# A hybrid decoder step on one core: another order of scaling, storing and loading in its last phase, ten weight chunks staged elsewhere, and sums moved to GpSimd

## The chip, the cores and the metric

The kernel runs on one core of one Trainium2 chip. The metric is the time of one execution in microseconds (us); smaller is better. Before the change three runs gave 2163.30, 2172.09 and 2173.16 us, so the median is 2172.09 us. PE is the matrix engine (TensorE), DVE is VectorE, ACT is ScalarE, POOL is GpSimd, and SP is SyncE, which in this kernel issues the DMAs. PEld is PE's weight load, SPq the queue of SP.

## The reference

One layer of a decoder with two branches on the same normalised input. 2048 new tokens and 8 sampling tokens pass through it. What the change touches is the end of it:

```python
def mixer_layer(x, ...):
    h = rmsnorm(x, g_pre)
    z = h @ w_in                                   # q, kv, z_att, u_pool, z_pool, g_att, g_pool
    o_lat = blocked_causal_mla(q_abs, q_r, pos, ckv_new, kr_new)
    o = jnp.einsum('bshr,rhv->bshv', o_lat, w_uv).reshape(b, L, ATT_WIDTH)
    y_att = (o * jax.nn.silu(z_att)) @ w_o_att
    p, pool_state = pool_mixer(u_pool, pool_hist, pos, w_pool, pool_scale)
    y_pool = (p * jax.nn.silu(z_pool)) @ w_o_pool
    merged = jax.nn.sigmoid(g_att) * y_att + jax.nn.sigmoid(g_pool) * y_pool
    x = x + merged @ w_out
...
y_prompt, y_sample = rmsnorm(xp, g_final), rmsnorm(xs, g_final)
```

D_MODEL is 1024, there are 8 heads of 128, and all is float32.

## The kernel before, in words

The core first makes the latents, queries and attention of all tokens, then the decode step of the 8 sampling tokens. The function `merge`, the subject of the change, does the rest in two further passes and a last one. Every engine has its own list of instructions, run in the order in which they are written; semaphores tie the lists together. Every float32 matrix product is made from three: an operand is split into a high part (a copy by ACT) and a low part (the difference, `split`, by DVE or POOL), and `three_products` multiplies high by high, high by low and low by high. A product over a depth of four blocks of 128 is thus 12 matmuls.

1. A first pass makes the gates and the pooling branch and stores them in memory (`zs`, `sa`, `sp`, `gp`).
2. The pass over **chunks** (variable `c`, five chunks of 412 tokens). A chunk has 24 units, slots 0 to 23. Slots 0 to 15 are the attention output product (kind `OA`, two units for each of eight tiles), slots 16 to 23 the pooling output product (kind `OP`, eight tiles `n`). A unit is 12 matmuls on 412 columns. Beside the units of chunk `c`, the values of chunk `c + 1` are made, a head at a time: a load of the head's latents (`olf`), high part on ACT, low part on POOL (`values_low`), a product of 3 matmuls, and a multiplication by the gate on DVE (`gated`), split in turn (`gat`). They start at slot `UV_AT`, 14, and take ten steps. After each `OP` unit DVE multiplies its result by the gate (`yp_ok`), and then adds the attention half (`m_ok`); SP stores the sum (`store_m`, to `mg`). Weights come three units ahead (`LEAD`), into six buffers.
3. The **join**: `mg` times the output weights, in eight groups `g` of 256 tokens, by one level of Strassen's scheme in Winograd's form, seven products `p` for each group where eight would be plain, and a tail of 8 tokens. `join_order` writes their order: (g,1), (g-1,4), (g-1,3), (g,2), (g,6), (g,5), (g,7) for each group, all of 12 matmuls on 512 columns. The right operands are 28 weight chunks `moved`, kept in SBUF for all groups; each comes by DMA into one of two buffers `moved_f`, and ACT and DVE split it (`high_moved`, `low_moved`). A few come during the last chunks, and from number 18 on after them: 18 and 19 at once, 20 to 27 with the first group's products (`JOIN_MOVED`). The left operands are the four rows `kept` of a group, made from staged rows of `mg` (three DMAs each, four sums on POOL in `staged_sums`, high part on ACT, low part on DVE).

The buffer `y` has two halves, for even and odd groups. `load_x` fills it with the input rows of a group; DVE adds the seven products into it (the first addition into it is at (g,5), line 2637); ACT makes its squares (`squares`, at (g,3)), POOL the inverse root (`rms`), DVE multiplies by it and by the final gain (`scale`, line 2531), and `store_y` stores it. `load_x(g)` needs the half that `store_y(g - 2)` reads, and waits for that store to land. DVE does `scale(g - 2)` at (g,6), SP issues `store_y(g - 2)` when it comes to (g,5) and `load_x(g)` when it comes to (g,7); it comes to a product when the one before it is complete. PE waits, before product (g,4), until ACT has copied the result of (g,7) out of PSUM (line 2330), and ACT waits for the addition of (g,5) before that, since both use the buffer `p1c`.

## Time and profile before

| | us |
|---|---|
| median of the runs | 2172.09 |
| the profiled execution | 2172.92 |
| its span (first to last instruction) | 2171.1 |
| PE busy in the span | 2025.3 |
| DVE, ACT, POOL busy | 1498.9, 1126.4, 511.8 |

The profile is of one execution. A span is the time from its first to its last instruction; here 1.8 us of the execution lie around it. A busy PE is not PE at its peak: its clock has two levels, and "PEclk" is the granted share of the full 2.4 GHz. In the 40 slices of the page PE is busy at nine tenths or more from the second to the 34th and then falls to six to eight tenths, while its clock falls from 9 tenths and more to 8 and 7; each slice is 54.3 us. The join begins at 1893 us.

### The profile page before, as it was taken

How to read it: one execution, taken by the hardware profiler on the slowest of the kernel's cores; microseconds unless marked ns; L12 is line 12 of the kernel's file. 1: busy time of each engine (PE TensorE's matmuls, PEld its weight loads, DVE VectorE, ACT ScalarE, POOL GpSimd, SP SyncE). 2: the span in 40 equal slices, each digit the busy share in tenths (PEclk: the TensorE clock that was granted, in tenths of full speed). 3: DMA queues.
4: the chain of work that ended last, by engine and by line, in shares of the span. 5: the costliest groups of instructions: out<-in, count | busy, mean ns of one | idle time of the engine just before them, and what ended most of it. 6: DMA issues, size and time to landing. Idle time of an engine off the chain costs nothing.

```text
span 2171.1 us, 37204 instructions
## 1 busy us (share of the span) xinstructions
PE 2025.3 (93%) x13077; PEld 1842.4 (85%) x13077; DVE 1498.9 (69%) x3208; ACT 1126.4 (52%) x2271; POOL 511.8 (24%) x647
## 2 busy tenths in 40 slices
PE   7999999999999999999999999999999999866666
PEld 6999888888888886899999999999998999855544
DVE  7877888888878775686687687587666777543333
ACT  5446766565555555556666666656633444332211
POOL 4444444333201102130040031021033111142210
PEclk9999999999999999999999999999999999988788
DMA  8876465344110313567767767768899988643232
GB/s 303 265 218 189 124 199 161 107 116 121 65 49 21 117 59 123 167 216 244 234 208 246 235 194 259 245 188 283 254 295 310 296 262 271 189 125 93 85 98 80
DMA packets 284249, 396.97 MB, mean 183 GB/s; under 512 B 34016, under 2 KB 152680, under 8 KB 283032
## 3 DMA queue, kind: packets, MB, share of 16 engines
q1 hardware_dynamic: 278272, 374.26, 55.7%
q0 software_dynamic: 2304, 12.58, 1.5%
q10 hardware_dynamic: 3488, 7.75, 1.1%
q8 instruction: 105, 1.72, 0.3%
q14 instruction: 80, 0.66, 0.1%
HBM read 295.77 MB, written 98.96 MB: 182 GB/s over the span
## 4 chain that ended last, share of the span: by engine, by line
PE 37%; DVE 10%; issue 7%; ACT 2%; DMA 2%; POOL 1%; SPq 0%; ACTq 0%; DVEq 0%; POOLq 0%
PE b_ps L131 37%; DVE d_wr L93 4%; ACT d_wr L1345 1%; DVE d_gat L93 1%; DVE d_spf L2602 1%; DVE d_saf L2608 1%; DVE d_pool L93 0%; DMA d_staged<-out_mg 0%; DMA d_quarters<-in_w_quarters 0%; DVE d_ht L93 0%; DVE d_pooled L2566 0%; DVE d_moved L93 0%; DMA d_zsf<-out_zs 0%; DMA d_moved_f<-out_w_moved 0%; DVE d_c L2551 0%
## 5 line engine op out<-in xcount | busy, mean ns | idle before, releaser
L93 DVE TENSOR_TENSOR d_wr<-d_ws,d_wr 128x512 fp32r<-128x512 f32 x568 | 429.2, 762 | 233.4 <-ACT d_wr L1345 227.1
L1345 ACT ACTIVATE d_wr<-d_ws 128x512 fp32r<-128x512 f32 x568 | 350.7, 628 | 281.1 <-PE b_ps L131 276.2
L131 PE MATMUL b_ps<-d_ht,d_wr 128*128 128x258 f32 x3072 | 399.1, 284 | 6.9 <-DVE d_wr L93 5.2
L131 PEld LDWEIGHTS b_ps<-d_ht,d_wr 128*128 128x128 f32 x3072 | 380.3, 189 | 13.8 <-DVE d_wr L93 12.2
L759 PE MATMUL b_ps<-kt,k_qs 128*128 128x512 f32 (+2 forms) x1520 | 337.8, 370 | 1.3 <-DVE b_p L1147 1.3
L131 PE MATMUL b_ps<-d_hb,d_wr 128*128 128x258 f32 x2304 | 302.8, 284 | 6.2 <-DVE d_wr L93 4.6
L759 PEld LDWEIGHTS b_ps<-kt,k_qs 128*128 128x128 f32 x1520 | 265.3, 188 | 49.0 <-DVE b_p L1147 4.3
L131 PEld LDWEIGHTS b_ps<-d_hb,d_wr 128*128 128x128 f32 x2304 | 287.5, 189 | 9.3 <-DVE d_wr L93 7.2
L1101 ACT ACTIVATE b_pt<-b_ps 128x512 fp32r<-128x512 f32 x272 | 158.5, 597 | 168.3 <-PE b_ps L1207 115.6
L93 DVE TENSOR_TENSOR b_pt<-b_ps,b_pt 128x512 fp32r<-128x512 f32 x272 | 183.0, 689 | 87.6 <-ACT b_pt L1101 86.5
L131 PE MATMUL b_ps<-d_moved,d_kept 128*128 128x512 f32 x672 | 173.7, 423 | 72.7 <-ACT d_p1c L2330 55.6
L131 PEld LDWEIGHTS b_ps<-d_moved,d_kept 128*128 128x128 f32 x672 | 136.9, 205 | 109.4 <-ACT d_p1c L2330 57.7
L1207 PE MATMUL b_ps<-b_pt,kv 128*128 128x512 f32 x816 | 227.8, 407 | 0.0
L1094 ACT ACTIVATE b_p<-b_p,b_bias 128x1024 f32<-128x1024 f32 (+7 forms) x192 | 171.6, 896 | 60.0 <-DVE b_low L1154 59.1
L131 PE MATMUL b_ps<-d_gat,d_wr 128*128 128x412 f32 x960 | 185.2, 354 | 7.5 <-DVE d_gat L93 7.5
L131 PEld LDWEIGHTS b_ps<-d_gat,d_wr 128*128 128x128 f32 x960 | 181.8, 191 | 10.1 <-issue 8.8
L1207 PEld LDWEIGHTS b_ps<-b_pt,kv 128*128 128x128 f32 x816 | 143.3, 189 | 24.2
L93 POOL TENSOR_TENSOR k_qs<-k_qf,k_qs 128x512 fp32r<-128x512 f32 (+1 forms) x52 | 71.2, 1370 | 358.8 <-issue 202.8
L1198 PE MATMUL b_ps<-ident,b_p 128*128 128x128 f32 x1088 | 149.2, 273 | 3.1 <-DVE b_p L1171 1.5
L1198 PEld LDWEIGHTS b_ps<-ident,b_p 128*128 128x128 f32 x1088 | 128.3, 140 | 25.6 <-DVE b_pt L93 3.2
L1147 DVE TENSOR_SCALAR_CACHE_REDUCE b_p<-b_ps 128x512 f32<-128x512 f32 (+1 forms) x192 | 125.2, 668 | 15.1 <-PE b_ps L759 13.0
L1171 DVE TENSOR_SCALAR b_p<-b_p,b_inverse 128x1024 f32<-128x1024 f32 (+7 forms) x192 | 133.3, 717 | 0.7
(246 smaller groups left out, 2557.5 us busy)
## 6 DMA issues: line engine op xcount, KB each, us to landing
d_ws<-out_w_sums SPq DMA_DIRECT2D x256, 256.0 KB, 3.5
d_ws<-in_w_pairs SPq DMA_DIRECT2D x192, 256.0 KB, 3.1
d_ws<-in_w_last SPq DMA_DIRECT2D x120, 256.0 KB, 4.1
b_quarters<-in_w_pairs SPq DMA_DIRECT2D x16, 1024.0 KB, 7.6
out_w_sums<-b_sums SPq DMA_DIRECT2D x16, 1024.0 KB, 10.0
out_q<-a_qout SPq DMA_DIRECT2D x32, 384.0 KB, 3.9
d_hf<-out_ht SPq DMA_DIRECT2D x32, 258.0 KB, 3.3
out_zs<-d_out SPq DMA_DIRECT2D x32, 258.0 KB, 4.2
```

The source lines that it names most:

```text
L93: return e.tensor_tensor(low, source, high.bitcast(f32), ALU.subtract)
L131: mm = pe.matmul(out, stationary(a, k), moving(b, k), start=first and k == 0 and a + b == 0, stop=last and k == depth - 1 and a == 1, skip ...
L759: mm = pe.matmul(out, qs[:, a, h, :], keep["kt"][:, first:first + size, b, :], start=k == 0, stop=k == len(pairs) - 1)
L1094: act.activation(span, span, ACT.Exp, bias=bias[:, at:at + 1], scale=-1.0 if negated else SCALE, accum_out=total[:, at, part:part + 1]).th ...
L1101: act.activation(pt[n % NPT][:, 0, :], ps_t[n % NTB][:, :], ACT.Copy).then_inc(pt_hi, 1)
L1147: dve.tensor_scalar(out, inp, 1.0, None, ALU.mult, ALU.max, accum_out=top[:, at, c:c + 1]).then_inc(s_sb, 1)
L1171: dve.tensor_scalar(span, span, inverse[:, at:at + 1], None, ALU.mult).then_inc(p_ok, 1)
L1198: mm = pe.transpose(ps_t[n % NTB][:, h * P:h * P + P], weights(u, h, slice(j * P, j * P + P)), ident[:, :])
L1207: mm = pe.matmul(ps_o[u % 2][:, :], kv[:, j, a, :], pt[n % NPT][:, b, :], start=j == 0 and k == 0, stop=j == tiles(u) - 1 and k == 2)
L1345: act.activation(ahead["wr"][s % WR][:, 0, :, :], ahead["ws"][s % WS][:, :, :], ACT.Copy).then_inc(ahead["w_hi"], 1)
L2602: dve.tensor_tensor(gate[:, :], bank[OP_BANK[a]][:, 0:T], gate[:, :], ALU.mult).then_inc(yp_ok, 1)
L2608: dve.tensor_tensor(saf[out_n][:, :], saf[out_n][:, :], gate[:, :], ALU.add).then_inc(m_ok, 1)
```

## The change

- **y and x.** DVE does `scale(g - 1)` at (g,5), in place of `scale(g - 2)` at (g,6). SP issues `store_y(g - 2)` when it comes to (g,1), in place of (g,5), and `load_x(g + 1)` when it comes to (g,4), in place of `load_x(g)` at (g,7). The fourth staged row of the next group is loaded at (g,2), in place of (g,6). POOL does `rms` after all four rows. The tail's load and split come earlier (at (7,2) and (7,6)).
- **Weight chunks.** Chunks 0 to 17 are loaded and split at the odd slots 1 to 11 of the third, fourth and fifth pass over a chunk. The last ten (in the order `RAW_ORDER`) are loaded without `moved_f`, each to a place of its own where `gat` lies, which is free once the last attention unit is done; they are loaded at slots 19 to 23 of the last chunk and split there and at (0,1). The four staged rows of group 0 come earlier.
- **Sums.** The 40 additions of the two gated halves go from DVE to POOL (`gated_sum`), each placed three steps behind a `values_low`; they are stored one slot later.
- **Value steps** begin at slot 13 (`UV_AT`), and the loads for them and the `quarters` loads come one slot earlier.

```diff
-UV_AT = 14
+UV_AT = 13
+RAW_ORDER = (21, 22, 23, 18, 19, 20, 24, 25, 26, 27)
...
-        STORE_M = {unit_slot(c, 20 + n): (c, n) for c in range(NC) for n in range(KD)}
+        STORE_M = {unit_slot(c, 21 + n): (c, n) for c in range(NC) for n in range(KD)}
-        LOAD_MOVED = {unit_slot(2, 4) + 4 * m: m for m in range(16)}
-        LOAD_MOVED |= {unit_slot(NC - 1, 17) + 2 * m: 16 + m for m in range(4)}
+        SPLIT_MOVED = {unit_slot(2 + m // 6, 1 + 2 * (m % 6)): m for m in range(12)}
+        SPLIT_MOVED |= {unit_slot(NC - 1, 1 + 2 * m): 12 + m for m in range(6)}
+        LOAD_MOVED = {s: m for s, m in SPLIT_MOVED.items()}
+        LOAD_STAGED = {unit_slot(NC - 1, at): i for i, at in enumerate((2, 4, 10, 12))}
+        SPLIT_STAGED = {unit_slot(NC - 1, at): i for i, at in enumerate((4, 6, 12, 14))}
+        LOAD_RAW = {unit_slot(NC - 1, 19 + k): (2 * k, 2 * k + 1) for k in range(5)}
+        SPLIT_RAW = {unit_slot(NC - 1, 21): (21,), unit_slot(NC - 1, 22): (22, 23), UNITS - 1: (18, 19, 20, 24)}
+        JOIN_RAW = {(0, 1): (25, 26, 27)}
...
+                if s in LOAD_RAW:
+                    if LOAD_RAW[s][0] == 0:
+                        sp.wait_ge(unit_ok, tile_slot(NC - 1, KD, 0))
+                        sp.wait_ge(moved_ok, MOVED_OK + 18)
+                    for n in LOAD_RAW[s]:
+                        load_raw(RAW_ORDER[n])
...
-            for q in range(2):
-                load_x(q)
+            load_x(0)
             for n, (g, p) in enumerate(JOIN):
                 sp.wait_ge(unit_ok, UNITS + n)
+                if p == 1 and 2 <= g < GROUPS_C:
+                    store_y(g - 2)
+                if p == 4 and 2 <= g + 1 < GROUPS_C:
+                    load_x(g + 1)
+                if (g, p) == (0, 6):
+                    load_x(1)
+                if p == 2 and g + 1 < GROUPS_C:
+                    load_staged(g + 1, 3)
...
-                if p == 5 and 2 <= g:
-                    store_y(g - 2)
-                if p == 7 and 2 <= g:
-                    load_x(g)
...
+            def high_raw(m):
+                act.wait_ge(raw_in, RAW_BASE + 16 * len(RAW_ORDER))
+                act.activation(moved[m][:, 0, :], raw[m][:, :], ACT.Copy).then_inc(moved_hi, 1)
...
+            def gated_sum(c, n):
+                pool.wait_ge(yp_ok, c * KD + n + 1)
+                pool.wait_ge(ya_ok, c * KD + n + 1)
+                pool.tensor_tensor(saf[n][:, :], saf[n][:, :], spf[n % 4][:, :], ALU.add).then_inc(m_ok, 1)
...
+                for h in range(KD + 3):
+                    if c < NC - 1 and h < NH:
                         values_low(c + 1, h)
+                    if h >= 3:
+                        gated_sum(c, h - 3)
...
-                            dve.tensor_tensor(saf[out_n][:, :], saf[out_n][:, :], gate[:, :], ALU.add).then_inc(m_ok, 1)
...
+                if p == 5 and g:
+                    scale(g - 1)
-                if p == 6 and 2 <= g < GROUPS_C:
-                    scale(g - 2)
```

How the rows of an engine move, at three places. The first is SP in the join, in a group in the middle. Before, a row of `mg` (lines 2035 to 2037), then the load of x (2053), the next row, and the store of y (2045):

```order
L2035 DMA d_staged_13156<-out_mg 128x128
L2036 DMA d_staged_13156<-out_mg 128x128
L2037 DMA d_staged_13156<-out_mg 128x256
L2053 DMA d_y_0_13148<-in_x 128x1024
L2053 DMA d_y_1_13149<-in_x 128x1024
L2035 DMA d_staged_13154<-out_mg 128x128
L2036 DMA d_staged_13154<-out_mg 128x128
L2037 DMA d_staged_13154<-out_mg 128x256
L2045 DMA out_y<-d_y_0_13150 128x1024
L2045 DMA out_y<-d_y_1_13151 128x1024
```

The same place after the change, where a row is lines 2049 to 2051, the store line 2059 and the load line 2067:

```order
L2049 DMA d_staged_13166<-out_mg 128x128
L2050 DMA d_staged_13166<-out_mg 128x128
L2051 DMA d_staged_13166<-out_mg 128x256
L2059 DMA out_y<-d_y_0_13160 128x1024
L2059 DMA out_y<-d_y_1_13161 128x1024
L2067 DMA d_y_0_13160<-in_x 128x1024
L2067 DMA d_y_1_13161<-in_x 128x1024
L2049 DMA d_staged_13164<-out_mg 128x128
L2050 DMA d_staged_13164<-out_mg 128x128
L2051 DMA d_staged_13164<-out_mg 128x256
```

The load of x now directly follows the store of the same half, both stand behind the first three rows of a group, and the fourth row stands behind them.

The second place is POOL in a chunk's pooling units. Before, the low parts of the values (line 93) stand alone; after, sums (line 2423) stand between them. Before:

```order
L93 TENSOR_TENSOR d_ols_13072<-d_olf_13081,d_ols_13072 128x412
L93 TENSOR_TENSOR d_ols_13073<-d_olf_13082,d_ols_13073 128x412
L93 TENSOR_TENSOR d_ols_13072<-d_olf_13083,d_ols_13072 128x412
L93 TENSOR_TENSOR d_ols_13073<-d_olf_13084,d_ols_13073 128x412
L2401 TENSOR_TENSOR d_changed<-d_quarters 128x512
```

After:

```order
L2423 TENSOR_TENSOR d_saf_13091<-d_saf_13091,d_spf_13074 128x412
L93 TENSOR_TENSOR d_ols_13072<-d_olf_13081,d_ols_13072 128x412
L2423 TENSOR_TENSOR d_saf_13092<-d_saf_13092,d_spf_13075 128x412
L93 TENSOR_TENSOR d_ols_13073<-d_olf_13082,d_ols_13073 128x412
L2423 TENSOR_TENSOR d_saf_13093<-d_saf_13093,d_spf_13076 128x412
L93 TENSOR_TENSOR d_ols_13072<-d_olf_13083,d_ols_13072 128x412
L2423 TENSOR_TENSOR d_saf_13094<-d_saf_13094,d_spf_13077 128x412
L93 TENSOR_TENSOR d_ols_13073<-d_olf_13084,d_ols_13073 128x412
```

Five of the eight sums of a chunk stand so, and three behind them.

The third place is SP near the end of the last chunk, after the change (line 2022 loads a gate, 2028 stores a sum, 2039 loads a raw weight chunk):

```order
L1338 DMA d_ws_12065<-in_w_last 128x512
L2039 DMA d_raw_13131<-out_w_moved 128x512
L2039 DMA d_raw_13132<-out_w_moved 128x512
L2022 DMA d_spf_13074<-out_sp 128x412
L2039 DMA d_raw_13133<-out_w_moved 128x512
L2039 DMA d_raw_13134<-out_w_moved 128x512
L2022 DMA d_spf_13075<-out_sp 128x412
L2028 DMA out_mg<-d_saf_13091 128x412
L2039 DMA d_raw_13135<-out_w_moved 128x512
L2039 DMA d_raw_13136<-out_w_moved 128x512
```

All ten raw loads stand ahead of the fourth of the eight stores; before, this stretch held single loads of `moved_f`, each of which needs the split of the chunk two before it.

## Rows read from the trace of the kernel before

**Rows 1.** Stretches: length, busy PE, PEld, DVE, ACT, POOL (x), PEclk, DMA share, GB/s
```profile
1826.50:1893.00 66.50, 58.62 (x290) 57.12 (x288) 41.93 (x65) 23.60 (x37) 9.25 (x16) 0.92 0.70 215
1893.00:1934.30 41.30, 24.75 (x85) 18.85 (x85) 14.12 (x21) 11.14 (x18) 8.32 (x16) 0.75 0.48 152
1934.30:1970.70 36.40, 36.39 (x156) 29.17 (x156) 18.70 (x21) 14.50 (x28) 17.80 (x35) 1.00 0.31 80
1970.70:2003.90 33.20, 21.10 (x84) 16.77 (x84) 11.32 (x13) 7.84 (x15) 7.94 (x19) 0.85 0.31 95
2037.30:2143.20 105.90, 63.78 (x240) 50.31 (x240) 32.16 (x39) 20.79 (x43) 18.04 (x44) 0.79 0.30 94
```

**Rows 2.** The chain that ended last, one period of the join (start, us, what)
```profile
1970.70 10.64 issue
1981.34 0.70 DVE d_y L2637
1982.15 0.61 ACT d_p1c L2330
1982.80 21.14 PE b_ps L131 x84
```

**Rows 3.** PE's waits in the join (total us, times, longest)
```profile
PE b_ps L131 <- ACT d_p1c L2330: 55.6, 5, 12.1
PE b_ps L131 <- DVE d_tail L93: 10.1, 1, 10.1
```

**Rows 4.** Timeline of SP's queue around one period of the join
```profile
1993.03 0.33 SPq L2035 DMA_DIRECT2D d_staged<-out_mg  x1
...
2001.53 1.49 SPq L2045 DMA_DIRECT2D out_y<-d_y  x2
...
2008.12 0.90 SPq L2053 DMA_DIRECT2D d_y<-in_x  x2
```

**Rows 5.** Timeline of DVE, same period
```profile
1991.46 2.08 DVE L93 TENSOR_TENSOR d_kept<-d_staged,d_kept 128x896 fp32r<-128x896 f32 x2
...
1999.17 1.09 DVE L93 TENSOR_TENSOR d_kept<-d_staged,d_kept 128x896 fp32r<-128x896 f32 x1 [2.78 <-ACT d_kept L2245]
2000.18 2.47 DVE L2531 SCALAR_TENSOR_TENSOR d_y<-d_y,d_stat,d_gfin 128x1024 f32<-128x1024 f32 x2
2013.88 0.69 DVE L2637 TENSOR_TENSOR d_y<-d_y,d_p1c 128x512 f32<-128x512 f32 x1 [11.23 <-issue]
...
2020.67 0.69 DVE L2644 TENSOR_TENSOR d_y<-d_y,b_ps 128x512 f32<-128x512 f32 x1 [3.87 <-PE b_ps L131]
2023.40 0.69 DVE L2646 TENSOR_TENSOR d_u2c<-d_u2c,b_ps 128x512 f32<-128x512 f32 x1 [2.04 <-PE b_ps L131]
```

**Rows 6.** Timeline of PE in the pass over chunks
```profile
1676.76 1.40 PE L131 MATMUL b_ps<-d_ols,d_wuv 128*128 128x412 f32 x3 [3.33 <-POOL d_ols L93]
...
1705.76 34.04 PE L131 MATMUL b_ps<-d_gat,d_wr 128*128 128x412 f32 x180 [1.50 <-DVE d_gat L93]
...
1767.76 35.48 PE L131 MATMUL b_ps<-d_gat,d_wr 128*128 128x412 f32 x180 [2.27 <-DVE d_gat L93]
```

**Rows 7.** Clock of the stretches after PE's 2.27 us wait (columns as Rows 1)
```profile
1767.70:1772.00 4.30, 4.24 (x15) 4.18 (x16) 1.46 (x3) 0.73 (x2) 0.00 (x0) 0.62 0.90 280
```

**Rows 8.** PE and DVE near the end of the last chunk, timeline
```profile
1878.60 13.79 PE L131 MATMUL b_ps<-d_gpl,d_wr 128*128 128x412 f32 x60 [5.01 <-DVE d_spf L2602]
...
1877.26 0.69 DVE L93 TENSOR_TENSOR d_moved<-d_moved_f,d_moved 128x512 fp32r<-128x512 f32 x1 [5.68 <-ACT d_moved L2239]
```

**Rows 9.** PE at the start of the join, timeline
```profile
1917.30 4.77 PE L131 MATMUL b_ps<-d_moved,d_kept 128*128 128x512 f32 x12 [12.79 <-ACT d_u2c L2327]
```

**Rows 10.** POOL and DVE in pooling units of the fourth chunk, timeline
```profile
1807.71 1.15 POOL L93 TENSOR_TENSOR d_ols<-d_olf,d_ols 128x412 fp32r<-128x412 f32 x1 [2.13 <-ACT d_ols L2230]
...
1807.84 1.47 DVE L2608 TENSOR_TENSOR d_saf<-d_saf,d_spf 128x412 f32<-128x412 f32 x1
...
1815.13 0.58 DVE L2608 TENSOR_TENSOR d_saf<-d_saf,d_spf 128x412 f32<-128x412 f32 x1
```

More of the change, by code:

```diff
@@ L1866, in merge @@
         moved_f = [at(where["gap"] + n * piece, f"moved_f{n}", [P, HALF]) for n in range(2)]
+        raw_at = {m: t_at[0] + (n * piece if n < 3 else 8 * NH * T - (len(RAW_ORDER) - n) * piece)
+                  for n, m in enumerate(RAW_ORDER)}
+        raw = {m: at(first, f"raw{m}", [P, HALF]) for m, first in raw_at.items()}
+        assert raw_at[23] + piece <= raw_at[18]
         gfin = at(where["gap"], "gfin", [P, D])
@@ L1910, in merge @@
         moved_in = [gp_out, sem("moved_in1")]
+        raw_in = moved_in[0]
         MOVED_BASE = (GP_BASE + 16 * NG * NAP, 0)
+        RAW_BASE = MOVED_BASE[0] + 16 * 9
         NG_ALL = NAP * PAIRS
@@ L2025, in load_moved, with load_raw @@
                 sp.dma_start(moved_f[m % 2][:, :], io[source][m % HD, part, :, :]).then_inc(moved_in[m % 2], 16)
+            def load_raw(m):
+                source, part = MOVED[m // HD]
+                sp.dma_start(raw[m][:, :], io[source][m % HD, part, :, :]).then_inc(raw_in, 16)
             def load_staged(q, i):
@@ L2158, in _ @@
+            load_staged(1, 2)
             for n in range(4):
                 sp.wait_ge(m_out[n], M_BASE[n] + 16 * 2 * NC)
[L2160 to L2161 removed]
+            load_x(0)
             for n, (g, p) in enumerate(JOIN):
                 sp.wait_ge(unit_ok, UNITS + n)
[L2164 to L2175 removed]
+                if p == 1 and 2 <= g < GROUPS_C:
[6 more added lines that the diff above has]
+                    load_staged(g + 1, 3)
+                if p == 7 and g + 2 < GROUPS_C:
+                    for i in range(3):
+                        load_staged(g + 2, i)
+                if (g, p) == (0, 7):
@@ L2315, in _ @@
                             high_staged(0, SPLIT_STAGED[s])
-            for m in (18, 19):
-                high_moved(m)
+                        for m in SPLIT_RAW.get(s, ()):
+                            high_raw(m)
             for n, (g, p) in enumerate(JOIN):
@@ L2442, in _ @@
                     change(k)
-                if c < NC - 1:
-                    for h in range(NH):
+                if c == NC - 1:
+                    for i in range(HD):
+                        staged_sums(0, i)
+                for h in range(KD + 3):
+                    if c < NC - 1 and h < NH:
                         values_low(c + 1, h)
+                    if h >= 3:
+                        gated_sum(c, h - 3)
             pool.memset(half_c[:, :], -0.5).then_inc(win_step, 1)
             pool.wait_ge(win_step, done[0] + 1)
-            for i in range(HD):
-                staged_sums(0, i)
-            for g in range(GROUPS_C):
+            for g in range(GROUPS_C + 1):
                 if g + 1 < GROUPS_C:
@@ L2453, in _ @@
                         staged_sums(g + 1, i)
-                        if i == 2 and g >= 2:
-                            rms(P, g % 2, 2, 4 * (g - 1), 3 * (g - 2))
-            for q in range(GROUPS_C - 3, GROUPS_C):
-                if q > GROUPS_C - 4:
-                    rms(P, q % 2, 2, 4 * q + 4, 3 * q)
+                if g:
+                    rms(P, (g - 1) % 2, 2, 4 * g, 3 * (g - 1))
             rms(TAIL_C, 0, 1, 4 * GROUPS_C + 2, 3 * GROUPS_C)
@@ L2512, in low_moved, with low_raw @@
                 split(dve, moved[m][:, 1, :], moved_f[m % 2][:, :], moved[m][:, 0, :]).then_inc(moved_ok, 1)
+            def low_raw(m):
+                dve.wait_ge(moved_hi, MOVED_HI + 18 + RAW_ORDER.index(m) + 1)
+                split(dve, moved[m][:, 1, :], raw[m][:, :], moved[m][:, 0, :]).then_inc(moved_ok, 1)
             def low_staged(q, i):
@@ L2617, in _ @@
                             low_staged(0, SPLIT_STAGED[s])
-            for m in (18, 19):
-                low_moved(m)
+                        for m in SPLIT_RAW.get(s, ()):
+                            low_raw(m)
             for n, (g, p) in enumerate(JOIN):
```

53 lines of the change are left out of this document (18 added, 35 removed).

## The prediction

> **What bounds the kernel now.** I read the page's slices first: PE is busy throughout until about 1850 us, so most of the span is bound by PE, and only the end is loose. The busy times by stretch say how loose: in the join's middle PE works 21 of 33 us at a granted clock of 0.85 and less, while DMA has a share of 0.3 and no other engine is half busy [rows 1]. So nothing is full there; something waits in a ring. The chain that ended last shows the ring, the same for each group: 10.6 us in which nothing visible runs, then DVE's first addition into y, ACT's copy of (g,7), and PE's 84 matmuls [rows 2]. PE's list of waits has five of them, 55.6 us, and a sixth before the tail, 10.1 us [rows 3]. What lies in the unnamed 10.6 us is read from two timelines: DVE scales y at 2000.18, SP stores it at 2001.53, x's load follows at 2008.12 and DVE's waiting addition starts at 2013.88 [rows 4, 5]. Store to load is 6.6 us, load to use 5.8 us: the DMA of y and x is the bound, begun too late for its group.
>
> Before the join, PE in the chunks waits 1.50 us twice and 2.27 us twice for the last low part of `gat` (two of them in the rows), 3.33 us once for POOL [rows 6], and 5.01 us in the last chunk for DVE, which waited 5.68 us for a weight chunk behind one of two `moved_f` buffers [rows 8]. Then 12.79 us at the join's start [rows 9].
>
> **Part 1, y and x (the middle of the join).** First what PE alone needs. Two results that DVE took up as soon as PE had them are 2.73 us apart [rows 5]; the stretch without the ring's wait has 13 products (156 matmuls) in 36.4 us, 2.80 each, at clock 1.00 [rows 1]. I take 2.75, or 19.25 us for a group. The 172.5 us from 1970.7 to 2143.2 hold 408 matmuls: 84 and 240 in the rows and 84 in a stretch between them like the first [rows 1]. That is 34 products, 93.5 us by 2.75. Freed: 79.0 us, and 1.4 us more because the tail's first matmuls, behind a wait too, run slowly.
>
> What is late next? Call the start of (g,1) zero. The scaling ends near 2 us (it stands behind (g-1,5) and takes 2.47 us [rows 5]); the store starts at 1 to 2 us, lands by 8 to 9, the load lands by 14 to 15; it is wanted at 16.5, when (g,5) ends. Slack 2 us. The other ring is the left operands. The fourth row of g+1 may load only when the first is split, 2.4 us after (g-1,3) ends (8.2). Before, from the issue of that load to the end of its low part took 7.2 us (1993.03 to 2000.26) [rows 4, 5], so the end is near 17.9, and PE wants it at 19.25. Slack 1.3 us, but x's load now is in flight beside it: I add 0.5 us a group over six groups, 3 us. The other end is 2 us a group, 12 us; below nothing is excluded, since PE has no less than its products to do. DVE needs about 12.5 us in 19, ACT 9. Part 1: minus 77.4.
>
> **Part 2, the join's start and the last chunk.** From 1893.0 to 1934.3 PE makes seven products in 41.3 us [rows 1]; 19.3 would do, 22.0 freed. SP has the ten raw loads issued before slot 23, so the first group waits for no `moved_f`. New there: ACT's copy of (0,6) stands behind the third staged row, about 1.2 us, and (1,1) needs the fourth row of group 1, which can load only when the first is split, about 2.3 us, with 1.5 us for a slower clock: 5 back, minus 17.0. The last chunk: 288 matmuls at 34.04/180 = 0.189 us [rows 6] are 54.5 of 66.5 us [rows 1], 12.0 freed, of which 3.7 belong to part 3. New: ACT's first raw copy waits for all ten loads. SP sends a pair per unit from the end of slot 16, since the gate loads between them want POOL's sums; the last pair goes about 12 us later and lands 3 to 5 us on, beside the end of slot 23. DVE's multiplication for slots 22 and 23 stands behind those splits, and PE wants it to start the join. 2.5 to 4.5 us; I take 4 with the clock. Its own ends are 0 (loads in time) and 10 (loads as slow as in the busiest stretches). Minus 4.3.
>
> **Part 3, the value steps one slot earlier.** The end of `gat` comes a unit (2.3 us) sooner, and PE waited at most 2.27 us for it: 7.5 us in four waits go. After 2.27 us the clock was 0.62 for 4.3 us [rows 7] and the 180 matmuls took 35.48 instead of 34.04 [rows 6]: 1.4 us more, twice, and a little in the others. Minus 10.5 (3.7 of them in the last chunk). The wait of 3.33 us stays: the `quarters` loads, POOL's work on them and the value steps all move by the same slot.
>
> **Part 4, the sums on POOL.** DVE is freed of 40 additions, and gains PE nothing, since no wait of PE on DVE in the pooling units is left to cut. POOL gets them. No row shows the operation there; the nearest has the same shape and two inputs in SBUF, 1.15 us [rows 10], and I take that. They stand between the low parts of the values, which PE waits for with about 0.4 us to spare. The two engines hinder each other: the addition on DVE that began while POOL worked took 1.47 us, one that did not 0.58 [rows 10], so it stood until POOL was done. If POOL's operations (2 of 1.15) and DVE's two with both inputs in SBUF (0.69 and 0.58) exclude each other in full, a pooling unit needs 3.57 us and PE gives it 2.82 (12 and 3 matmuls). Starts stand closer than durations, 0.5 us apart for one of 0.58, so 3.2 is nearer. 0.4 us over 5 units less 0.4 us spare, four times, is 6 us; I take 5. Ends: 0 (PE's spare takes it all) and 13 (0.75 over 5 units, less the spare, four times). Below nothing is excluded as PE has nothing to win.
>
> The Trainium skill (SBUF — State Buffer, "SBUF: two separate sides") says that this pair of ports is an exclusive lock, held for the whole instruction, between GpSimd and a VectorE operation with two SBUF inputs. By that rule in full, the sum would be the upper end, 13 in place of 5; the row of 1.47 us agrees with the blocking, and no row here shows it for the sums. The skill's GPSIMD Engine Reference, "Engine selection", would leave elementwise sums on VectorE, as about twice as slow on GpSimd; 1.15 beside 0.58 us agrees, but PE does not wait on that difference alone.
>
> **The sum.** Span 2171.1 - 79.0 - 1.4 + 3 - 22.0 + 5 - 8.3 + 4 - 10.5 + 5 = 2066.9. With 1.8 us around the span 2068.7: about 2069, 4.8% less. The profiled execution, 2172.92, lies 0.8 us above the median of the runs, so nothing is to be converted.
>
> **Rivals.**
> A, 2087 us: POOL and DVE exclude each other in all eight pooling units of four chunks, 0.75 us x 32 = 24 in place of 5. For it, [rows 10]; against it, three of eight sums come after the last low part, where PE waits for nothing of POOL.
> B, 2082 us: the row chain and x's load stretch the join's period from 19.75 to 22, over six groups 13.5 us. For it, a slack of 1.3 us and a load of 1 MB beside it; against it, DMA share 0.3 [rows 1].
> C, 2120 us: the wait for x only shrinks. If store and load come one product later than I have them and each lands 3 us later, 8 us of 10.6 stay in each of six periods, 48 us and a lower clock. Against it, 6.6 and 5.8 us were measured with rows of `mg` in flight too.
> D, slower than before: a POOL sum in the value steps takes over 4.8 us. Place: the pooling units of four chunks; price: 1.15 + x - 2.82 us in each of 32 units; at x = 4.8 that is 100 us, the whole of the gain. The nearest rows exclude it nearly: POOL's 1.15, and DVE's longest in these units, 1.47.
> E, about 2048: none of my new waits comes (3 + 5 + 4 + 5 less what the clock gives back) and the 3.33 us wait goes.
>
> **How the numbers follow.** Forecast 0.62; A 0.12; B 0.12; C 0.03; D 0.02; E 0.09. The forecast's time is 2069. The range goes from 2050 (just over E) to 2092 (past A and B), with C, D and part of E left out, as are sums of A and B. A measurement of this kernel tells about 0.5% from nothing, 11 us. All cases but D are far beyond that: faster 0.96, same 0.02, slower 0.02.
>
> **What would show it.** Right: in the join's middle PE runs without a wait over 2 us, at clock 1.00, a period of 19 to 20 us; DVE's first addition into y never waits for a DMA; no wait of PE on `gat`; a wait of some us between slot 22 and the first product of the join, behind raw chunks; POOL's sums near 1.15 us. Wrong: a wait at (g,5) of several us (C); PE waiting for POOL's low parts in each pooling unit (A); PE waiting for `kept` before (g,1) (B). If PE's clock stayed at 1.2 GHz through the join, a product would take 4.8 us as the one after the long wait did [rows 9], and 56 products would give back all that is won; no busy stretch in the rows shows that, so it has no chance of its own.

## The result, and the profile after

The changed kernel took 2078.78 us (median of 4 runs, 2075.72 to 2079.02), the kernel before 2169.73 us beside it (4 runs). The ratio is 0.9581, with a 95% interval of 0.9555 to 0.9607: 4.2% less. The forecast was 2069 us and 4.8% less, so some 10 us are missing by the time and 13 us by the ratio. The profiled execution took 2075.72 us with a span of 2073.9; the prediction's sum for the span was 2066.9, so there 7.0 us are missing. Two single executions understate the miss: the profiled one before took 3.2 us more than its median, and the one after took 3.1 us less.

From the page of the changed kernel, busy times and the clock in 40 slices:

```profile
PE 2003.5 (97%) x13077; PEld 1826.2 (88%) x13077; DVE 1502.1 (72%) x3168; ACT 1123.6 (54%) x2271; POOL 586.5 (28%) x687
PEclk9999999999999999999999999999999999999999
```

PE is now busy for 97% of the span and its clock no longer falls at the end. PE's timeline in the join (start, us, what, waits in brackets) answers to [rows 3, 9]:

```profile
1891.18 13.88 PE L131 MATMUL b_ps<-d_moved,d_kept 128*128 128x512 f32 x48 [5.96 <-DVE d_spf L2638]
1906.81 3.04 PE L131 MATMUL b_ps<-d_moved,d_kept 128*128 128x512 f32 x12 [1.75 <-ACT d_u2c L2352]
1911.23 136.39 PE L131 MATMUL b_ps<-d_moved,d_kept 128*128 128x512 f32 x588 [1.39 <-DVE d_kept L93]
```

The join starts at 1891.18 us. The six long waits are gone: from (1,1) on, 588 matmuls, 49 products, follow each other without one, 2.78 us each. The ring of y as DVE and SP show it in a middle group, to be laid beside [rows 4, 5]:

```profile
1968.85 0.69 DVE L2669 TENSOR_TENSOR d_y<-d_y,d_p1c 128x512 f32<-128x512 f32 x1
1969.45 2.68 DVE L2567 SCALAR_TENSOR_TENSOR d_y<-d_y,d_stat,d_gfin 128x1024 f32<-128x1024 f32 x2
...
1975.52 0.69 DVE L2676 TENSOR_TENSOR d_y<-d_y,b_ps 128x512 f32<-128x512 f32 x1 [2.05 <-PE b_ps L131]
```
```profile
1971.71 0.85 SPq L2059 DMA_DIRECT2D out_y<-d_y  x2
1976.22 0.81 SPq L2067 DMA_DIRECT2D d_y<-in_x  x2
```

The first addition into y (L2669) waits for nothing, where it waited 11.23 us; the scaling stands behind it. The next store of y is issued at 1991.29, so a group takes about 19.5 us.

The two profiles split the span at the join's first product. From there to the end before took 2171.1 - 1893.07 = 278.0 us, after takes 2073.9 - 1891.18 = 182.7: minus 95.3, where the sum had 77.4 + 17.0 = 94.4. Ahead of it the change gained 1.9 us, where the sum had 4.3 + 10.5 - 5 = 9.8. So the whole miss lies ahead of the join. The 1.9 us are no gain of the change at all. The last rows of the pass before the chunks, which the change does not touch, are in the two profiles:

```profile
1572.69 1.70 PE L131 MATMUL b_ps<-d_ht,d_wr 128*128 128x258 f32 x12 [0.57 <-ACT d_p L2269]
```
```profile
1570.33 1.69 PE L131 MATMUL b_ps<-d_ht,d_wr 128*128 128x258 f32 x12 [0.57 <-ACT d_p L2294]
```

The changed kernel's execution was 2.4 us ahead here already. That is the spread of single executions: e6 below has the same instructions up to the join and stands at 1573.30. From these rows to the join's first product is called the pass below; it took 320.4 us before and 320.9 us after, so the pass over chunks gained nothing. PE's waits there, grouped (total us, times, longest), from 1590 to 1911 us of the changed kernel, and the same of the kernel before:

```profile
PE b_ps L131 <- POOL d_ols L93: 10.5, 3, 7.9
PE b_ps L131 <- DVE d_spf L2638: 7.0, 5, 6.0
PE b_ps L131 <- DVE d_wr L93: 2.9, 3, 1.1
PE b_ps L131 <- ACT d_u2c L2352: 1.8, 1, 1.8
PE b_ps L131 <- DVE d_gat L93: 1.3, 4, 0.3
```
```profile
PE b_ps L131 <- DVE d_gat L93: 7.5, 4, 2.3
PE b_ps L131 <- DVE d_spf L2602: 5.7, 2, 5.0
PE b_ps L131 <- POOL d_ols L93: 4.3, 4, 3.3
```

The waits on `gat` went, 6.2 us. In their place stand 6.2 us more on POOL and 2.9 us on weights. The longest of them, where [rows 6] has 3.33:

```profile
1678.29 1.40 PE L131 MATMUL b_ps<-d_ols,d_wuv 128*128 128x412 f32 x3 [7.88 <-POOL d_ols L93]
```

What is behind it is read on POOL, where lines 2432 to 2437 make `changed` from `quarters`, and on SP:

```profile
1652.64 2.94 POOL L2433 TENSOR_TENSOR d_changed<-d_quarters 128x512 f32<-128x512 f32 x1
...
1670.95 1.27 POOL L2432 TENSOR_TENSOR d_changed<-d_quarters 128x512 f32<-128x512 f32 x1 [11.97 <-DMA d_quarters<-in_w_quarters]
...
1676.74 2.52 POOL L93 TENSOR_TENSOR d_ols<-d_olf,d_ols 128x412 fp32r<-128x412 f32 x2
```
```profile
1643.88 0.61 SPq L2156 DMA_DIRECT2D d_quarters<-in_w_quarters  x1
...
1650.27 0.38 SPq L2015 DMA_DIRECT2D d_saf<-out_sa  x1
1659.01 0.37 SPq L2161 DMA_DIRECT2D out_w_moved<-d_changed  x1
1659.43 2.15 SPq L1338 DMA_DIRECT2D d_ws<-in_w_last  x1
...
1663.05 0.38 SPq L2156 DMA_DIRECT2D d_quarters<-in_w_quarters  x1
```

It is a ring of its own, `quarters` load, POOL's four operations, store, next load, and only then the low parts of the values, which stand behind it on POOL. The slots of the load and the store are lower bounds: SP reached the third load at 1643.88, the kernel before issued it at 1644.03 (its row: `1644.03 0.38 SPq L2142 ... d_quarters`). Counted from the start of the pass (1570.33 and 1572.69), the third load came 2.2 us later than before (73.6 against 71.3) though its slot is one earlier, the fourth 4.8 us later, and the low part began 3.9 us later (1676.74 after, 1675.21 before). PE wanted it 0.7 us earlier (at 1678.29 - 7.88 = 1670.41 after, 1676.76 - 3.33 = 1673.43 before). Together these are the 4.55 us by which the wait grew. While SP stood at the store, from 1650.7 to 1659.0, the weight loads behind it stood too; no wait of PE for weights is seen between 1638 and 1678 us. The chain that ended last names the link, in both kernels:

```profile
1663.05 7.83 DMA d_quarters<-in_w_quarters
```
```profile
1660.61 8.64 DMA d_quarters<-in_w_quarters
```

### The profile page after: what moved, and what is told of

Its sections match the earlier page's. It is cut to its first block, busy times and chain, and to the rows that moved or that the text cites. A ratio compares the mean times of both kernels' runs of the same rounds, so it can differ in the third digit from the quotient of the medians.

```text
span 2073.9 us, 37208 instructions
## 1 busy us (share of the span) xinstructions
PE 2003.5 (97%) x13077; PEld 1826.2 (88%) x13077; DVE 1502.1 (72%) x3168; ACT 1123.6 (54%) x2271; POOL 586.5 (28%) x687
## 4 chain that ended last, share of the span: by engine, by line
PE 36%; DVE 10%; issue 4%; DMA 3%; ACT 2%; POOL 2%; SPq 1%; ACTq 0%; DVEq 0%; POOLq 0%
PE b_ps L131 36%; DVE d_wr L93 4%; DVE d_gat L93 2%; ACT d_wr L1345 1%; DMA d_zsf<-out_zs 1%; DMA d_quarters<-in_w_quarters 1%; DVE d_spf L2638 1%; DVE d_pool L93 0%; POOL d_ols L93 0%; POOL d_saf L2423 0%; DMA d_staged<-out_mg 0%; DVE d_pooled L2602 0%; DVE d_c L2587 0%; DVE d_ht L93 0%; DMA d_olf<-out_olat 0%
## 5 line engine op out<-in xcount | busy, mean ns | idle before, releaser
L131 PE MATMUL b_ps<-d_hb,d_wr 128*128 128x258 f32 x2304 | 302.7, 284 | 6.2 <-DVE d_wr L93 4.6
L131 PE MATMUL b_ps<-d_moved,d_kept 128*128 128x512 f32 x672 | 159.1, 399 | 9.1 <-DVE d_spf L2638 6.0
L131 PEld LDWEIGHTS b_ps<-d_moved,d_kept 128*128 128x128 f32 x672 | 127.9, 191 | 40.1 <-DVE d_spf L2638 6.3
```

Of the source, the lines that this page charges most:

```text
L131: mm = pe.matmul(out, stationary(a, k), moving(b, k), start=first and k == 0 and a + b == 0, stop=last and k == depth - 1 and a == 1, skip ...
```

## The experiments

Four theories were at stake: that the `quarters` ring, and not GpSimd's new work, made the 7.88 us; that the sums cost what was said; that the wait ahead of the join comes from ACT's place for the raw copies; and what each part is worth alone. Differences are taken between ratios (to before, timed on the same chip) and multiplied by 2169 us; "join at" is the start of its first product in the profile, and "pass" the time from the start of the pass over chunks to it, which leaves out what the executions differ in before. Even so the pass of one and the same order varies: e6 is the changed kernel up to the join, and its pass is 1.9 us longer.

| kernel | median us | ratio | 95% interval | join at | pass |
|---|---|---|---|---|---|
| before | 2169.73 | 1 | | 1893.07 | 320.4 |
| changed | 2078.78 | 0.9581 | 0.9555-0.9607 | 1891.18 | 320.9 |
| e1: y and x only | 2090.72 | 0.9637 | 0.9611-0.9663 | 1891.81 | 321.3 |
| e7: earlier value steps only | 2171.86 | 1.0011 | 1.0000-1.0023 | 1889.64 | 318.4 |
| e12: y and x, weight chunks | 2067.84 | 0.9544 | 0.9531-0.9557 | 1884.36 | 313.6 |
| e3: changed, sums on DVE | 2073.20 | 0.9553 | 0.9529-0.9576 | 1888.37 | 316.5 |
| e2: changed, value steps at 14 | 2085.36 | 0.9609 | 0.9587-0.9631 | 1901.23 | 328.5 |
| e6: changed, x at (g,7) | 2089.90 | 0.9632 | 0.9616-0.9648 | 1896.03 | 322.7 |
| e4: changed, quarters early | 2069.69 | 0.9534 | 0.9512-0.9556 | 1885.86 | 314.0 |
| e5: changed, raw splits late | 2074.88 | 0.9559 | 0.9544-0.9575 | 1890.55 | 319.1 |
| e8: e4 and e5 | 2064.06 | 0.9524 | 0.9511-0.9537 | 1881.31 | 309.0 |
| e9: e4, e5 and e3 | 2058.31 | 0.9490 | 0.9473-0.9506 | 1872.25 | 300.0 |
| e10: e9, rows in another order | 2061.18 | 0.9506 | 0.9493-0.9519 | 1875.71 | 302.7 |
| e13: e9, value steps at 14 | 2064.49 | 0.9531 | 0.9518-0.9544 | 1878.57 | 308.3 |

**e1, y and x alone.** The kernel before with the first part of the change: `scale(g - 1)` at (g,5), `store_y(g - 2)` at (g,1), `load_x(g + 1)` at (g,4), the fourth row at (g,2), `rms` after all rows.

```diff
+                if p == 1 and 2 <= g < GROUPS_C:
+                    store_y(g - 2)
+                if p == 4 and 2 <= g + 1 < GROUPS_C:
+                    load_x(g + 1)
```

> The kernel before with part 1 alone: scaling at (g,5), store of y at (g,1), load of x at (g,4), the fourth row at (g,2), the inverse root after all four rows. Theory (the late load of x made the ring of the join, and PE's stalls were all of it): 77 to 80 us less than before, about 2090 to 2094 us, no wait over 2 us between 1970 us and the tail. Rival (half of the gain of the join comes from the weight chunks' new place, through DMA and ACT): 40 us less, about 2130 us, with waits left in the middle groups.

Measured 0.9637, minus 79 us of 2169 (78 by the medians). PE's waits ahead of the join were those of before (`gat` 7.5 us in four). The term of 77.4 stands.

**e6, x's load back at (g,7).** The changed kernel, with one statement moved.

```diff
-                if p == 4 and 2 <= g + 1 < GROUPS_C:
-                    load_x(g + 1)
+                if p == 7 and 2 <= g < GROUPS_C:
+                    load_x(g)
```

> The changed kernel, but x of a group is loaded where it was before, at (g,7), 13.6 us later than in the change; scaling and store stay early. By the prediction x is wanted when (g,5) ends, so x, landing about 5.8 us after the end of (g,5), would cost nearly 6 us in each of six groups, 35 us and slower clocks: 2115 us or more. Theory now (the addition of x stands in front of ACT's copy of (g,7), and PE needs that copy only before (g,4), two products later, so about 5 us of the lateness are free): 1 to 3 us a group, 2085 to 2097 us. Rival (the load was never the bound once the store is early): no change, 2079 us.

Plus 0.0051, 11 us, with waits of PE of this kind, one or two in a group:

```profile
1958.66 3.03 PE L131 MATMUL b_ps<-d_moved,d_kept 128*128 128x512 f32 x12 [1.25 <-ACT d_p1c L2355]
...
1979.90 20.19 PE L131 MATMUL b_ps<-d_moved,d_kept 128*128 128x512 f32 x84 [1.09 <-ACT d_p1c L2355]
```

So a load five products later makes waits of only 1 to 1.3 us; a group takes 21.2 us in place of 19.5 (the two rows are one group apart). PE needs the addition of (g,5) by (g,4), two products behind the point that the prediction took for the need; the slack was larger than its 2 us.

**e12, y and x and the weight chunks.** The changed kernel with the sums on DVE and `UV_AT` and its loads back by one slot, so parts 1 and 2 alone.

```diff
-UV_AT = 13
+UV_AT = 14
...
-                    if h >= 3:
-                        gated_sum(c, h - 3)
```

> The changed kernel with the sums back on VectorE and the value steps, their loads and the quarters loads one slot later: of the change only the order of y and x and the weight chunks are left. Theory: this part alone is worth about 17 us on top of the 78 of the first, and the value steps at slot 13 are worth nothing in its company either: 2073 us, waits of PE on gat of 1.5 to 2.3 us four times back and the POOL wait in the second chunk short (about 3). Rival, the prediction's own term: the earlier value steps are worth 7 to 10 us once the other parts are in, so this kernel takes 2081 us or more, and the weight chunks are worth only about 10.

0.9544: 20 us less than e1 (the intervals leave some 6 us either way), the prediction's 17.0 + 4.3 = 21.3 for part 2. And it is faster than the whole change: by 0.0037, 8 us give or take 6, so parts 3 and 4 together cost something. The POOL wait was 4.22 us. The waits on `gat` were 1.50 to 1.59 us, four times, where before and e1 have 2.27 us in the last two chunks; here is the one that was followed by 35.48 us of matmuls before [rows 6], and below it what stood in DVE's list ahead of those splits in the kernel before:

```profile
1764.43 34.04 PE L131 MATMUL b_ps<-d_gat,d_wr 128*128 128x412 f32 x180 [1.50 <-DVE d_gat L93]
```
```profile
1758.83 1.27 DVE L93 TENSOR_TENSOR d_moved<-d_moved_f,d_moved 128x512 fp32r<-128x512 f32 x1
```

The split of a weight chunk lay between the pooling units, DVE worked without a pause from it to the last `gat` split, and part 2 moves it to an odd slot from 1 to 11. So part 2 took 0.8 us of wait and 1.4 us of slower matmuls out of this chunk (35.48 - 34.04) that the prediction had booked for part 3.

**e7, the earlier value steps alone.** Before, with `UV_AT` 13 and the four tables of loads one slot earlier.

```diff
-UV_AT = 14
+UV_AT = 13
...
-        LOAD_QUARTERS = {unit_slot(k // 2, 4 if k % 2 == 0 else 9): k for k in range(HD)}
+        LOAD_QUARTERS = {unit_slot(k // 2, 3 if k % 2 == 0 else 8): k for k in range(HD)}
```

> The kernel before with part 3 alone (value steps from slot 13, their loads and the quarters loads one slot earlier). Theory: the four waits on gat go (7.5 us and 2 to 3 us of clock), and PE's wait for POOL in the second chunk grows from 3.3 to about 7 us: 4 to 7 us less than before, ratio 0.997. Rival (the growth of that wait belongs to the sums on POOL or to the weight chunks): it stays near 3.3 us and the kernel is 10 us faster, ratio 0.995.

1.0011, no gain. The waits on `gat` are gone, but one row tells of the 7.88 us of the changed kernel, with the sums on DVE:

```profile
1676.45 1.40 PE L131 MATMUL b_ps<-d_ols,d_wuv 128*128 128x412 f32 x3 [7.86 <-POOL d_ols L93]
```

The long wait belongs to the slot, not to the sums. Here PE wanted the low part 3.4 us earlier in the pass than before, and POOL began it 1.1 us later (at 1674.90). The profile's pass is 2.0 us shorter, which the ten timed runs don't show.

**e4, the third `quarters` load earlier.** It goes from slot 3 of the second chunk to slot 22 of the first; nothing else changes.

```diff
-        LOAD_QUARTERS = {unit_slot(k // 2, 3 if k % 2 == 0 else 8): k for k in range(HD)}
+        LOAD_QUARTERS = {unit_slot(0, 3): 0, unit_slot(0, 8): 1, unit_slot(0, 22): 2, unit_slot(1, 8): 3}
```

> The changed kernel, but the third quarters load (for chunk 1) is issued at slot 22 of chunk 0 in place of slot 3 of chunk 1; all else the same. Theory (SP stands 8.7 us at the store of the changed quarters because their load came late, and the weight loads and the fourth quarters load stand behind it): the store no longer holds SP, the wait of 7.9 us before a value product falls under 2 us, 6 to 9 us faster, about 2070 to 2073 us. Rival (DMA is full there and the wait stays, whatever the order): no change, 2077 to 2079 us.

0.9534, 10 us less, give or take 7 (9.1 by the medians), from one number in a table:

```profile
1672.93 0.84 PE L131 MATMUL b_ps<-d_ols,d_wuv 128*128 128x412 f32 x3 [1.35 <-POOL d_ols L93]
```

7.88 became 1.35, and the 15 matmuls behind the wait, which had taken some 1.5 us longer at a granted clock of 0.64, now ran at 1.00. SP did not stand at the store any more: it issued the store at 1653.20, right behind the entry ahead of it, and the fourth load at 1656.50. This shows the cause of the long wait: the time of the third load. The buffer ring and the queue that stands were freed by the same edit, so what each of them costs is not separated.

**e3, the sums back on DVE.** The changed kernel without part 4.

```diff
+                        if kind == "OP":
+                            dve.wait_ge(yp_ok, c * KD + out_n + 1)
+                            dve.wait_ge(ya_ok, c * KD + out_n + 1)
+                            dve.tensor_tensor(saf[out_n][:, :], saf[out_n][:, :], gate[:, :], ALU.add).then_inc(m_ok, 1)
...
-                        gated_sum(c, h - 3)
```

> The changed kernel with part 4 undone: the 40 sums are on DVE again, at the place they had, all else as changed. By the prediction the sums on POOL cost 5 us: 2074 us. By what PE's waits in the changed trace add up to in the pooling units (1.1 us once, 0.2 to 0.3 us a few times) it is 1 to 3 us: 2076 to 2078 us. Rival (DVE needed the relief once the value steps and weight splits came closer together): slower than the changed kernel, 2082 us or more, with PE waiting on gat or on weights.

0.9553 against 0.9581: the sums on POOL cost 6 us here (5.6 by the medians), the prediction's 5. The intervals overlap, so this pair alone doesn't settle it; e8 against e9 (below) gives 7 and their intervals do not. Groups by line (out<-in, count | busy us, mean ns | idle before) from 1590 to 1890 us show how. The changed kernel:

```profile
L2423 POOL TENSOR_TENSOR d_saf<-d_saf,d_spf 128x412 f32<-128x412 f32 x39 | 57.2, 1468 | 32.6 <-DVE d_spf L2638 32.5
L93 DVE TENSOR_TENSOR d_gat<-d_gated,d_gat 128x412 fp32r<-128x412 f32 x32 | 44.4, 1388 | 3.0 <-ACT d_gat L2250 2.7 <-DMA d_zsf<-out_zs 0.3
```

e3:

```profile
L93 DVE TENSOR_TENSOR d_gat<-d_gated,d_gat 128x412 fp32r<-128x412 f32 x32 | 20.6, 642 | 1.1 <-ACT d_gat L2250 1.1
```

The part relieved DVE of 40 sums of 0.69 us (27.6 us) and lengthened 32 other operations of DVE by 0.75 us (24 us). (0.69 us is the mean; the median of e3 is 0.58 us.) A unit of the changed kernel, in rows of its POOL and DVE:

```profile
1633.49 1.45 POOL L2423 TENSOR_TENSOR d_saf<-d_saf,d_spf 128x412 f32<-128x412 f32 x1 [1.64 <-DVE d_spf L2638]
...
1636.58 1.45 POOL L2423 TENSOR_TENSOR d_saf<-d_saf,d_spf 128x412 f32<-128x412 f32 x1 [1.64 <-DVE d_spf L2638]
```
```profile
1633.93 1.46 DVE L93 TENSOR_TENSOR d_gat<-d_gated,d_gat 128x412 fp32r<-128x412 f32 x1
...
1637.02 1.46 DVE L93 TENSOR_TENSOR d_gat<-d_gated,d_gat 128x412 fp32r<-128x412 f32 x1
```

Both run beside each other at 1.46 us, the split ends 0.45 us after the sum, and the unit takes 3.09 us on these two engines where PE needs 2.82. The exclusive lock between GpSimd and a VectorE operation with two SBUF inputs, of which the Trainium skill (SBUF — State Buffer, "SBUF: two separate sides") tells, agrees with these rows: the split alone takes 0.58 us, with a sum on POOL 1.39 on the mean.

The waits of PE that e3 does not have are small, though: 1.3 us for `gat` and 1.0 us for the gated result (L2638), in eight waits of 0.23 to 0.33 us. Behind the 7.88 us no wait for POOL's low parts is seen at all. So the rows name some 2.3 of the 6 us, and where PE loses the rest is not shown.

**e2, the value steps back at slot 14, sums on POOL.**

```diff
-UV_AT = 13
+UV_AT = 14
```

> The changed kernel with part 3 undone (value steps from slot 14, their loads and the quarters loads one slot later). My theory of the miss: the earlier value steps buy back four waits on gat (about 10 us with the clock) and pay at the second chunk, where PE waits 7.9 us for POOL's low part since the quarters loads could not come earlier. Then undoing brings the gat waits back and the one wait down to 3.3 us: 4 to 7 us slower than the changed kernel, about 2083 us. Rival (the 7.9 us wait comes from the sums on POOL, not from the slot): it stays near 8 us here, and the kernel is 10 us or more slower, about 2089 us.

0.9609: 6 us more than the changed kernel, with overlapping intervals; the pass is 7.6 us longer. The waits on `gat` were not the 1.5 to 2.3 us of before, but 3.85 to 3.87 us four times, of which this is one:

```profile
1712.08 35.43 PE L131 MATMUL b_ps<-d_gat,d_wr 128*128 128x412 f32 x180 [3.87 <-DVE d_gat L93]
```

At slot 14 the sums cost 14 us (0.9609 against 0.9544 of e12, intervals apart), at slot 13 six. The rows account for the 14: four waits longer by 2.3 us, and 35.43 us for 180 matmuls where e12 has 34.02. So part 3 gained only what part 4 had added to the waits that it removes.

**e5, the raw splits behind the last slot.** ACT's raw copies wait for all ten loads; here none stands ahead of slot 23's work.

```diff
-        SPLIT_RAW = {unit_slot(NC - 1, 21): (21,), unit_slot(NC - 1, 22): (22, 23), UNITS - 1: (18, 19, 20, 24)}
+        SPLIT_RAW = {UNITS - 1: (21, 22, 23, 18, 19, 20, 24)}
```

> The changed kernel, but the splits of the raw chunks 21, 22 and 23 stand at slot 23 behind DVE's last multiplication, in place of slots 21 and 22 before it. Theory (PE waits 6.0 us at the join's start only because DVE's last two multiplications are queued behind splits that need all ten raw loads): the wait falls to about 1 us, 3 to 5 us faster, about 2074 to 2076 us. Rival (the raw chunks themselves are late, and the join needs them or what stands behind them): the wait turns up at the third to fifth product, and the time stays at 2078 us or so.

0.9559, 5 us less by the ratio and 3.9 by the medians, with overlapping intervals. The trace is clear on the wait:

```profile
1890.55 11.43 PE L131 MATMUL b_ps<-d_moved,d_kept 128*128 128x512 f32 x48 [0.68 <-DVE d_spf L2638]
1906.04 19.12 PE L131 MATMUL b_ps<-d_moved,d_kept 128*128 128x512 f32 x71 [4.06 <-ACT d_u2c L2352]
```

5.96 became 0.68, and the first four products took 11.43 us instead of 13.88, since the clock did not fall (granted 1.00 in this stretch, 0.81 in the changed kernel's). Inside the first group nothing is gained: its first product to (1,1) still takes about 20 us, now with 4.06 us ahead of (0,7).

**e9, all three stops removed.** e4, e5 and e3 together.

> The changed kernel with three edits: the third quarters load at slot 22 of chunk 0, the raw splits behind the last multiplication, the sums on DVE. If the three causes are separate, the gains add up (9.1, 4 and 5.6 us): about 2060 us, and this would be the fastest of all. If two of them share a wait (the start of the second chunk, or DVE's queue at the join's start, where the sums of the last slots are DVE's again), 2063 to 2068 us.

0.9490, 2058.31 us, the fastest kernel. Relative to the changed one 0.0091, 20 us; the three alone give 10 + 5 + 6 = 21. They add up, within the 7 us that the intervals leave.

**e8, the same with the sums on POOL.**

> As the fastest kernel so far (third quarters load early, all raw splits behind the last slot), but with the gated sums on GpSimd as in the change. Theory: the sums' cost does not depend on the other two stops, 5 to 7 us: 2064 to 2065 us, with waits of PE of about 1 us on gat or wr spread over the chunks. Rival: part of the 5.6 us measured before was the same time as the quarters wait, hidden here, and the kernel takes 2060 us or less.

0.9524 against 0.9490, intervals apart: 7 us for the sums, as much as beside the long wait, so the two were not the same time.

**e10, another order of ACT's rows in the first group.** e9 with one entry moved.

```diff
-        JOIN_STAGED = {(0, 1): (0, 1), (0, 2): (2,), (0, 6): (3,)}
+        JOIN_STAGED = {(0, 1): (0, 1), (0, 6): (2, 3)}
```

> As the fastest kernel so far, but in the first group ScalarE copies the third staged row at (0,6) instead of (0,2), so that its copy of (0,6), for which PE waits 4.0 us before (0,7), stands ahead of it. Theory: the rows are the bound themselves (the fourth needs the split of the first, then a load and a sum on GpSimd), so the wait only moves one product on, to (1,1), and the time stays within 1 us of 2058. Rival: the place in ScalarE's order is the bound, and 3 to 4 us go: 2054 to 2055 us.

No gain: 0.9506, plus 3.5 us with overlapping intervals. The wait ahead of (0,7) shrank from 4.04 us and one ahead of (1,1) came:

```profile
1888.60 3.02 PE L131 MATMUL b_ps<-d_moved,d_kept 128*128 128x512 f32 x12 [1.46 <-ACT d_u2c L2352]
1895.10 137.98 PE L131 MATMUL b_ps<-d_moved,d_kept 128*128 128x512 f32 x588 [3.48 <-DVE d_kept L93]
```

The wait has moved one product on, as expected of rows that are late whatever ACT does first. In the profiles the stretch from the join's start on took 183.7 us against 182.5 of e9; the other 2.7 us lie in the pass, where the two kernels are the same. So the rival's gain of 3 to 4 us did not come. The expected "within 1 us" can be neither confirmed nor denied by the timed runs.

**e13, e9 with the value steps at slot 14.** Does part 3 pay once the ring is out of its way?

> As the fastest kernel so far (sums on VectorE, third quarters load early, raw splits late), but with the value steps and their loads one slot later again. Theory: the earlier value steps gain their four waits on gat only when the quarters load no longer holds GpSimd; here it does not, so this kernel loses against the fastest one: four waits of 1.5 us come back, 6 to 8 us in all, 2065 us. Rival: the earlier value steps are worth nothing in any company, because the time returns in waits for weight chunks and at the join, and this kernel takes 2058 to 2060 us.

0.9531 against e9's 0.9490, intervals apart: here the earlier slot is worth 9 us by the ratio, 6.2 by the medians. The sum is the expected one, its parts are not. Three waits on `gat` are of 1.50 us, but the first is this:

```profile
1640.30 36.46 PE L131 MATMUL b_ps<-d_gat,d_wr 128*128 128x412 f32 x180 [5.09 <-DVE d_gat L93]
```
```profile
1636.43 1.71 POOL L2435 TENSOR_TENSOR d_changed<-d_quarters,d_changed 128x512 f32<-128x512 f32 x1
1638.22 1.49 POOL L2437 TENSOR_TENSOR d_changed<-d_quarters,d_changed 128x512 f32<-128x512 f32 x1
```
```profile
1636.94 1.64 DVE L2642 TENSOR_TENSOR d_saf<-d_saf,d_spf 128x412 f32<-128x412 f32 x1
1638.51 1.64 DVE L93 TENSOR_TENSOR d_gat<-d_gated,d_gat 128x412 fp32r<-128x412 f32 x1
```

POOL's work on the early quarters now lies beside the last `gat` of the chunk, and the sum and the split take 1.64 us each where they take 0.58. So 3.6 us of wait, and 2.4 us more for the 180 matmuls behind it (34.02 where the wait was 1.50), are a collision of this pair of edits and not the value of the slot, which is then nearer 3 us by the ratio and near nothing by the medians (an estimate: 9 or 6.2, less 6.0).

## Why the prediction was right or wrong

The forecast gained 77.4 + 21.3 + 10.5 - 5 = 104.2 us. By the timed ratios the parts gave 79 + 20 - 2 - 6 = 91 us. Of the 13 us between them the third term accounts for 12.5; the others are off by 1 to 1.6 us each, less than such a difference can be off by (some 6 us).

- **The join's middle (minus 77.4): right.** e1 alone measured 79. Three sizes in it were off without weight. A product takes 2.78 us, not 2.75. The 0.5 us a group for the row chain did not come; 7 x 2.78 is the whole period. The slack of x's load was taken as 2 us at (g,5), and e6 showed that PE needs its result two products later.
- **Weight chunks (minus 21.3 in two stretches): right in the sum.** e12 less e1 is minus 20. In the profiles 16.6 of it lie in the join (said 17.0) and 7.7 ahead of it (said 4.3). Ahead of it the part did something that was not forecast of it: it shortened the waits on `gat` in the last two chunks. The join's first seven products now end near 1911.23 + 5.6 = 1916.8, 25.6 us from its start, where 24.3 were forecast: the waits of 1.75 and 1.39 us are the 1.2 and 2.3 that were named. The wait between slots 22 and 23 and the join is 5.96 us, and 8.4 with the slower matmuls behind it, for a priced 4 with the clock, while its removal in e5 gained 4 to 5; the cause was the one given, as e5 shows.
- **Value steps one slot earlier (minus 10.5): wrong, and this is the step that failed.** The waits on `gat` fell as said, to 0.3 us each. "The wait of 3.33 us stays: the `quarters` loads, POOL's work on them and the value steps all move by the same slot" did not hold: the loads moved in the table, but in the pass the third came 2.2 us later (1.1 earlier in e7) and the fourth 4.8 us later (2.2 in e7), PE's demand moved earlier, and 3.33 us became 7.88. The 10.5 was also counted against the kernel before and not against parts 1 and 2: with these in, e12 still had 6.1 us of waits on `gat` to remove and no slower matmuls behind them. Smaller waits came too: for POOL in the first chunk 2.6 us (0.6 before), for weights 2.9 us (none before; 0.3 to 1.0 in the kernels with slot 14, 2.3 to 5.1 in those with slot 13 and parts 1 and 2). The part alone gave plus 2 (e7); on top of parts 1 and 2 it gave plus 2 (e3 less e12, within what can be measured), instead of minus 10.5. With the ring out of the way it gave minus 9 (e9 less e13), some 6 of that by a collision. The passes of the profiles say the same, to about 2 us: against the kernel before, parts 1 and 2 gave minus 6.8 (e12; said minus 4.3), part 3 on top plus 2.9 (e3; said minus 10.5) and part 4 plus 4.4 (said 5), in sum plus 0.5 where minus 9.8 was forecast. That the profiled execution missed by 7.0 us only is in part luck: 2.4 us of it came before the pass.
- **Sums on POOL (plus 5): right in size, the mechanism in part.** Plus 6 (e3) and plus 7 (e8 less e9). The price of one was low, 1.47 us on the mean for 1.15 forecast. A unit of 3.09 us was measured where 3.2 was taken. But the prediction had PE wait for POOL's low parts, and the waits that the rows name are for DVE's splits and gated results, some 2.3 us; the rest of the 6 is not located, so the size may be right in part by luck. That part 3 and part 4 act on the same waits was not seen: at slot 14 the sums would have cost 14.
- **Rivals.** A, exclusion in all eight pooling units, at 24 us: excluded, since the sums cost 6 to 7 here, and 14 at slot 14. B, a join period of 22 us, and C, the wait for x only shrinks: excluded, no wait in 49 products. D: POOL's sums were never above 1.63 us. E needed the 3.33 us wait to go; it grew.
- The chain of waits of the kernel before had the link already, `1660.61 8.64 DMA d_quarters`, right ahead of the wait that the prediction left alone. A value step that is moved has to be followed back to that load, not to its number in the table.

Open: the waits on POOL in the first chunk, 1.52 and 1.12 us, stand behind the second `quarters` load by the chain (`1595.47 6.45 DMA d_quarters`), and no run moved that load; e9 has 0.28 us there for a reason not found. Where the waits for weights come from was not tried either. And what e9 still waits for at (0,7), 4.04 us behind the staged rows, was only moved by e10.

## What to carry to other kernels

A number in a table of slots says when an instruction may be issued; where the queue, a buffer's ring or a store that waits stands ahead of it, it doesn't move with the table. Before a consumer is put earlier, follow its producers through the chain of waits and check that each has slack of its own. And parts of a change that shorten the same wait must be costed together: the earlier slot was worth nothing with the sums on DVE and the old `quarters` load, and some 6 us with the sums on POOL. A single profile of each kernel is not enough to split a gain of a few us by stages: first compare them at a point up to which both run the same instructions.
